# Hybrid decoder trunk on one Trainium2 core: the last norm's weights go into the gate matrix, and the low halves move to GpSimd

## The reference, cut to what matters

```python
def rms_norm(x, g):
    xf = x.astype(jnp.float32)
    y = xf * lax.rsqrt(jnp.mean(xf * xf, axis=-1, keepdims=True) + EPS)
    return (y * g.astype(jnp.float32)).astype(x.dtype)
...
        h = h + moe_out.reshape(bsz, s, d)
        u = rms_norm(h, norm_ple_g[l])
        ple_gate = jax.nn.sigmoid((u @ w_ple_gate[l]).astype(jnp.float32)).astype(h.dtype)
        h = h + ple_gate * (p[l] @ w_ple[l])
    return rms_norm(h, final_norm_g)
```

## Time and profile before

| what | value |
|---|---|
| three timed runs | 902.76, 903.9, 904.63 us (median 903.9) |
| profiled execution, its own time | 903.69 us |
| its span in the profile | 901.9 us |
| PE busy | 845.4 us, 94% of the span |
| DVE, ACT, POOL busy | 338.2, 262.3, 86.7 us |
| HBM | 247.41 MB read, 286 GB/s over the span |
| tail, from the first restore (827.1) to the end of the last product (894.5) | 67.4 us |

### The profile page before, as it was taken

How to read it: one execution, slowest core, us unless ns; L and a number is a source line. 1 busy time by engine, 2 the same in 40 slices (tenths; PEclk the granted TensorE clock), 3 DMA queues, 4 the chain that set the end, 5 groups by cost and what they waited for, 6 DMA issues and landing times.

```text
span 901.9 us, 10174 instructions
## 1 busy us (share of the span) xinstructions
PE 845.4 (94%) x4223; PEld 526.7 (58%) x4223; DVE 338.2 (37%) x462; ACT 262.3 (29%) x372; POOL 86.7 (10%) x63
## 2 busy tenths in 40 slices
PE   4999899999999999899999999888998897998896
PEld 3778687778888888635535344352352343533585
DVE  6699518952762526511110110101100101014975
ACT  7565326633432326302010100101001001013646
POOL 3429470000000000000000000000000000000000
PEclk9999999999999999999999999999999998999999
DMA  9222222211523772999999999999999999998802
GB/s 259 88 94 93 94 94 94 93 47 47 187 93 134 298 301 79 377 430 427 409 423 430 428 427 427 426 429 428 426 427 428 428 427 428 429 420 316 303 0 94
DMA packets 44758, 254.37 MB, mean 282 GB/s; under 512 B 8676, under 2 KB 9768, under 8 KB 31912
## 3 DMA queue, kind: packets, MB, share of 16 engines
q1 hardware_dynamic: 42120, 248.47, 68.2%
q0 software_dynamic: 2304, 4.20, 1.2%
q10 hardware_dynamic: 288, 1.05, 0.3%
HBM read 247.41 MB, written 10.49 MB: 286 GB/s over the span
## 4 chain that ended last, share of the span: by engine, by line
PE 68%; DMA 17%; DVE 10%; ACT 2%; issue 2%; SPq 1%; DVEq 0%; ACTq 0%
PE bank L1301 66%; DMA ring<-in_w_down_e_dram 11%; DMA ring<-in_w_up_e_dram 3%; DMA ring<-in_p_dram 2%; DVE ring L1007 1%; DVE ring L1011 1%; DVE r L1234 1%; SPq L461 1%; PE bank L1500 1%; DVE r L1013 1%; DMA r<-in_x_dram 1%; PE bank L1314 1%; DVE ring_rounded L382 0%; DVE r L1239 0%; DVE r L945 0%
## 5 line engine op out<-in xcount | busy, mean ns | idle before, releaser
L1301 PE MATMUL bank<-ring_rounded,ring_rounded 128*128 128x512 f32 x736 | 250.8, 395 | 3.7 <-DVE ring_rounded L953 3.7
L1301 PE MATMUL bank<-r_rounded,ring_rounded 128*128 128x512 f32 x736 | 243.8, 399 | 4.8 <-DVE ring_rounded L382 2.8
L1301 PEld LDWEIGHTS bank<-r_rounded,ring_rounded 128*128 128x128 f32 x736 | 139.5, 190 | 38.0 <-DVE ring_rounded L382 3.6
L1301 PEld LDWEIGHTS bank<-ring_rounded,ring_rounded 128*128 128x128 f32 x736 | 139.8, 190 | 35.3 <-issue 6.3
L1301 PE MATMUL bank<-ring,gain 128*64 128x512 f32 x472 | 118.0, 603 | 8.5 <-issue 4.9
L1301 PE MATMUL bank<-ring,hT 128*64 128x512 f32 x400 | 113.8, 628 | 6.4 <-DMA ring<-in_w_down_e_dram 6.4
L1301 PE MATMUL bank<-ring,junk 128*64 128x512 f32 x472 | 115.4, 592 | 0.0
L655 POOL DMA_INDIRECT expert_rows<-r,row_i x16 | 15.6, 977 | 674.1 <-DVE r L1200 398.3
L1301 PEld LDWEIGHTS bank<-ring,gain 128*64 128x64 f32 x472 | 35.5, 138 | 75.9 <-issue 67.7
L1301 PEld LDWEIGHTS bank<-ring,junk 128*64 128x64 f32 x472 | 37.0, 137 | 72.1 <-issue 72.0
L1301 PEld LDWEIGHTS bank<-pick,r_rounded 128*128 128x128 f32 x576 | 72.6, 199 | 9.9 <-issue 8.5
(11 more groups left out here) (204 smaller groups left out, 729.8 us busy)
## 6 DMA issues: line engine op xcount, KB each, us to landing
ring<-in_w_up_e_dram SPq DMA_DIRECT2D x31, 2048.0 KB, 29.0
ring<-in_w_gate_e_dram SPq DMA_DIRECT2D x25, 2048.0 KB, 27.4
ring<-in_w_down_e_dram SPq DMA_DIRECT2D x22, 2048.0 KB, 31.9
ring<-in_w_in_dram SPq DMA_DIRECT2D x18, 1024.0 KB, 7.3
r<-in_w_down_e_dram SPq DMA_DIRECT2D x5, 2048.0 KB, 33.0
r<-in_w_gate_e_dram SPq DMA_DIRECT2D x5, 2048.0 KB, 28.1
ring<-in_w_down_e_dram SPq DMA_DIRECT2D x7, 1024.0 KB, 21.9
r<-in_x_dram SPq DMA_DIRECT2D x8, 512.0 KB, 8.0
```

The source lines that it names most:

```text
L1301: return nc.tensor.matmul(*a, **k)
```

## The change

It does six things, all in the tail.

1. The stream itself is transposed, without the norm. Its root factor becomes the `scale` operand of the sigmoid, one per token, and DVE takes one reciprocal for all four tiles instead of four. The four passes of `normalise` over 128x1024 go.
2. The norm's weights are multiplied into the gate matrix: quarters 0 and 1 by ACT (four `Copy` with a scale per partition each, ahead of `gate_high`), quarters 2 and 3 by POOL (one multiply of 128x2048 each). For that the rows of the matrix are laid out as `(p k)` instead of `(k p)`, and the transposes read the stream with the same stride. The weights now come as 128x8 (`gain_col`) instead of 128x1024.
3. The low parts of quarters 0 and 1 are taken by POOL instead of DVE. Those of quarters 2 and 3 stay with DVE.
4. SP loads `p` ahead of `w_ple`, and quarter 1 right behind quarter 0, ahead of the scatter's end. PE waits for `p` and for `w_ple` separately.
5. The products of `p` use four banks instead of six, and the first stream transposes stand between product 5 and product 6.
6. In the last loop the squares of the first halves come one product later, and one `tensor_scalar` serves all four tiles. The results are written where the first expert outputs lay.

The diff, cut to its core:

```diff
         def ple_bank(q):
-            return bank[q % 6]
+            return bank[q % 4]
...
-            wg = w_ple_gate[0].rearrange("(k p) n -> p k n", p=P)
+            wg = w_ple_gate[0].rearrange("(p k) n -> p k n", p=P)
...
-                    sp.dma_start(wple, w_ple[0].rearrange("(k p) n -> p k n", p=P)).then_inc(ple_in, 16)
-                    sp.dma_start(p_rows, p[0, 0].rearrange("(i p) n -> p i n", p=P)).then_inc(ple_in, 16)
+                    sp.dma_start(p_rows, p[0, 0].rearrange("(i p) n -> p i n", p=P)).then_inc(p_in, 16)
+                    sp.dma_start(wple, w_ple[0].rearrange("(k p) n -> p k n", p=P)).then_inc(wple_in, 16)
                     wait_expert_read(max(range(8, 3 * NE, LEAD)))
                     load_gate(0)
+                    load_gate(1)
...
-                if i == 1:
-                    load_gate(1)
...
# POOL, behind the expert loop
+            for step in range(2):
+                gate_low(pool, nc.gpsimd, step, first_low_ready)
+            for step in range(2, 4):
+                h, ks = gate_steps[step]
+                pool.wait_ge(pg_in[step], 16)
+                nc.gpsimd.tensor_tensor(gate_part("whole", h)[:, ks, :], gate_part("whole", h)[:, ks, :],
+                                        gain_col[:, ks].unsqueeze(2).to_broadcast([P, KD // 2, HALF]),
+                                        ALU.mult).then_inc(pg_scaled, 1)
...
# ACT
             def gate_high(step):
                 h, ks = gate_steps[step]
-                act.wait_ge(pg_in[step], 16)
+                if step < 2:
+                    act.wait_ge(gain_in, 32)
+                    act.wait_ge(pg_in[step], 16)
+                    for k in range(ks.start, ks.stop):
+                        whole_k = gate_part("whole", h)[:, k, :]
+                        ins = nc.scalar.activation(whole_k, whole_k, ACT.Copy, scale=gain_col[:, k:k + 1])
+                    after(ins)
+                else:
+                    act.wait_ge(pg_scaled, step - 1)
...
-            for q in range(4):
+            for q in range(3):
                 copy_ple(q)
-            norm_h2(0)
+            gate_high(1)
+            copy_ple(3)
+            copy_h2T(0)
             copy_ple(4)
             copy_ple(5)
-            norm_h2(1)
+            norm_h2(0)
             copy_ple(6)
             copy_ple(7)
-            gate_high(1)
-            copy_u3T(0)
+            norm_h2(1)
+            copy_h2T(1)
+            norm_h2(2)
+            norm_h2(3)
             gate_high(2)
-            copy_u3T(1)
-            norm_h2(2)
+            copy_h2T(2)
+            gate_sigmoid(0)
             gate_high(3)
-            copy_u3T(2)
-            norm_h2(3)
-            copy_u3T(3)
+            copy_h2T(3)
...
# DVE
             add_y(0)
             add_y(1)
-            dve.wait_ge(gain_in, 32)
-            normalise_u3(0)
-            gate_low(dve, v, 0)
-            normalise_u3(1)
-            split_u3(0)
-            gate_low(dve, v, 1)
+            split_h2(0)
             add_y(2)
-            split_u3(1)
-            normalise_u3(2)
             add_y(3)
-            split_u3(2)
-            normalise_u3(3)
-            gate_low(dve, v, 2)
-            split_u3(3)
-            gate_low(dve, v, 3)
-            dve.wait_ge(h2_ready, TT)
+            split_h2(1)
+            dve.wait_ge(std_done, 2 * TT)
+            v.reciprocal(rstd[:, 2 * TT:3 * TT], std[:, 2 * TT:3 * TT]).then_inc(h2_rstd_ready, 1)
+            gate_low(dve, v, 2, second_low_ready)
+            split_h2(2)
+            gate_low(dve, v, 3, second_low_ready)
+            split_h2(3)
...
# PE
+            for q in range(6):
+                ple_product(q)
+            transpose_h2(0)
+            ple_product(6)
+            ple_product(7)
             for q in range(2 * TT):
                 ple_gate(q)
```

More of the change, by code:

```diff
@@ L575, in _ @@
                 sp.wait_ge(final_ready, q + 1)
-                sp.dma_start(out[0, i * P:(i + 1) * P, part], u3[:, i, part]).then_inc(stored, 16)
+                sp.dma_start(out[0, i * P:(i + 1) * P, part], result(i)[:, part]).then_inc(stored, 16)
             sp.wait_ge(stored, 16 * 2 * TT)
@@ L888, in norm_h2, with copy_h2T, gate_sigmoid @@
                 norm(2 * TT + i, h1[:, i, :])
[L890 to L894 removed]
+            def copy_h2T(i):
+                copy_transposed(2 * (TT + i), h2T_high, (4, 5, 6, 7))
+                copy_transposed(2 * (TT + i) + 1, h2T_high, (4, 5, 6, 7))
+            def gate_sigmoid(q):
+                act.wait_ge(pg_psum, q + 1)
+                if q == 0:
+                    act.wait_ge(h2_rstd_ready, 1)
+                if q >= 2:
+                    act.wait_ge(h3_ready, q - 1)
+                n = 2 * TT + q % TT
+                nc.scalar.activation(psig[:, q % 2, :], bank[q % 4][:, :], ACT.Sigmoid, scale=rstd[:, n:n + 1]).then_inc(pg_sig, 1)
@@ new lines, in _ @@
+            copy_h2T(3)
+            for q in range(1, TT):
+                gate_sigmoid(q)
+                first_square(q - 1)
+            first_square(TT - 1)
+            for q in range(TT, 2 * TT):
+                i, n = q % TT, 2 * TT + q
+                gate_sigmoid(q)
+                after(nc.scalar.activation(std[:, n:n + 1], eps[:, :], ACT.Sqrt))
+                act.wait_ge(h3_ready, q + 1)
+                after(nc.scalar.activation(junk[:, HALF:D], h1[:, i, HALF:D], ACT.Square, accum_out=ssq[:, i:i + 1]))
+                act.wait_ge(half_bias, 1)
+                nc.scalar.activation(std[:, n:n + 1], ssq[:, i:i + 1], ACT.Sqrt, bias=rstd[:, i:i + 1],
+                                     scale=1.0 / D).then_inc(std_done, 1)
@@ L1584, in _, with transpose_h2, ple_product, ple_gate @@
             ins.then_inc(pT_psum, 1)
-            def transpose_u3(i):
-                transpose_rows(2 * (TT + i), u3, (4, 5, 6, 7))
-                transpose_rows(2 * (TT + i) + 1, u3, (4, 5, 6, 7))
+            def transpose_h2(i):
+                pe.wait_ge(h2_ready, i + 1)
+                for h in range(2):
+                    q = 2 * i + h
+                    if q >= 4:
+                        pe.wait_ge(ut_low, 2 * TT + q - 3)
+                    for k in range(4):
+                        ins = nc.tensor.transpose(bank[4 + q % 4][:, k * P:(k + 1) * P], h1_by_k(i)[:, 4 * h + k, :], ident[:, :])
+                    ins.then_inc(ut_psum, 1)
+            def ple_product(q):
+                i, h = q // 2, q % 2
+                if q >= 4:
+                    pe.wait_ge(ple_ready, q - 3)
+                for k in range(KP):
+                    ins = mm(ple_bank(q)[:, :], pT[:, k, i * P:(i + 1) * P], wple[:, k, h * HALF:(h + 1) * HALF],
+                             start=(k == 0), stop=(k == KP - 1))
+                ins.then_inc(ple_psum, 1)
+            def ple_gate(q):
+                h, i = q // TT, q % TT
+                pe.wait_ge(ut_low, 2 * (TT + i + 1))
+                if q < TT:
+                    pe.wait_ge(ple_ready, TT + q + 1)
+                else:
+                    pe.wait_ge(pg_sig, q - 3)
+                cols = slice(i * P, (i + 1) * P)
+                for k in range(KD):
+                    if k == KD // 2 and q < TT - 1:
+                        transpose_h2(q + 1)
+                    if i == 0 and k % (KD // 2) == 0:
+                        pe.wait_ge((first_low_ready, second_low_ready)[h], k // (KD // 2) + 1)
+                    wh, wl = gate_part("high", h)[:, k, :], gate_part("low", h)[:, k, :]
+                    for p_, (still, stream) in enumerate(((h2T_high, wh), (h2T_high, wl), (h2T_low, wh))):
+                        ins = mm(bank[q % 4][:, :], still[:, k, cols], stream, start=(k == 0 and p_ == 0),
+                                 stop=(k == KD - 1 and p_ == 2))
+                ins.then_inc(pg_psum, 1)
             pe.wait_ge(y_stored, rounds * NE + 2)
@@ L1593, in _ @@
             pe.wait_ge(pT1_ready, 1)
[L1594 to L1624, removed]
+            pe.wait_ge(wple_in, 16)
+            for q in range(6):
[3 more added lines that the diff above has]
+            ple_product(7)
             for q in range(2 * TT):
-                if q == 0:
-                    pe.wait_ge(ple_ready, 2 * TT)
                 ple_gate(q)
```

63 lines of the change are left out of this document (26 added, 37 removed).

## The result

The changed kernel takes 910.66 us (median of five runs, 910.46 to 913.5) against 903.9 before: the ratio is 1.0083, with a 95% interval of 1.0064 to 1.0103. It is slower, by 6.8 us. The profiled execution took 910.92 us with a span of 908.8, against 903.69 and 901.9.

What follows compares the result with a forecast made beforehand. DVE was taken to set when the gate products start, PE the end from there. The profiled 903.69 us plus 8.3 for the later second product and 0.1 for the scaled sigmoid gave 912.1 us, range 906 to 916.5.

Steps and rivals of the forecast that it cites:

- DVE sets the start of the products, PE the end: In the tail, DVE decides when gate products start; from 846.5 us on PE is full and sets the end.
- POOL and DVE exclude each other, and all four passes hit: Tail: each POOL pass shuts out a DVE operation with two SBUF inputs; four passes cost 17.0 us; chance 0.68.
- the sum: DVE's path to the second gate product: 826.5 + 8.2 + 9.84 + 17.04 + 1.29 = 862.9 us.
- The case at 55.80: Mixing stage before the change: DVE's L1011 takes 4.95 us beside a POOL pass, 0.69 without; read as exclusion.
- The operation at 19.32: Before the change: a DVE operation on eight columns takes 1.57 us, ending with POOL's pass; read as exclusion.
- 4.26 us a pass: Cost to DVE of each POOL pass in the tail, taken as 4.95 - 0.69; four passes cost 17.0 us.
- Restores from 826.5: DVE's restores start at 826.5 us instead of 827.1, waiting for POOL to release the row buffer behind its last scatter.
- The second product at 862.9: Second gate product on PE starts at 862.9 us against 854.6 before, 8.3 us later.
- the dearest rival: Exclusion costs 5.16 us a pass and one more low-clock stretch adds 1.7: 917.4 us; chance 0.10.
- DVE keeps its place while it has work: Rival: POOL gets in only where DVE waits; third product starts 5.4 us later, 909.2 us; chance 0.12.
- No exclusion: Rival: POOL's tail passes don't block DVE; third product starts 3.2 us earlier, 900.6 us; chance 0.10.
- Behind the second product: Third product at 869.2 us finds its quarter 2 ready at 868.5; quarter 3 and the rest hide behind products.

Runs made afterwards that it cites:

- d_reads: The kernel before plus eight POOL multiplies of 128x1024 behind the last scatter, results unused: 916.81 us, ratio 1.0149.
- e_writes: The kernel before plus 18 POOL memsets of 128x1024 behind the last scatter, results unused: 902.93 us, ratio 0.9998.
- h_lows_only: The kernel before with only the low parts of quarters 0 and 1 moved from DVE to POOL: 908.71 us, ratio 1.0047.
- g_reordered: The changed kernel without POOL passes in the tail, ACT's quarter 2 work ahead of two norms, further ACT and DVE reordering: 900.69 us, ratio 0.9975.
- b_scale_act: The changed kernel with quarters 2 and 3 scaled by ACT instead of POOL: 910.34 us, ratio 1.0072 to the kernel before.
- f_loads: The kernel before with only the load order changed (p ahead of w_ple, quarter 1 right behind quarter 0): 905.18 us, ratio 1.0011.

## Why the prediction was right, point by point

- **DVE sets the start of the products, PE the end.** Right. Everything behind the start of the second product cost the same as before but for its first twelve matmuls and 0.1 us of the sigmoid.
- **POOL and DVE exclude each other, and all four passes hit.** Right, and shown apart from all else by d_reads and e_writes. Four long operations were forecast, and there are four. But they are not the ones that I had named. The two low parts were to hit the third and fourth restore; the restores were done by then, and all four passes hit adds. Besides the earlier restores (below), the first low part began a little late, at 833.09 and not at 832.3, since ACT's scaled copies waited for `gain_col` up to 828.51. That changed nothing in the sum, since all of these stand ahead of tile 1's low part. It did change PE's idle time: the first stream transposes waited 2.77 us and not some 8, as only one pass stood ahead of tile 0's adds.
- **What the rows of before showed.** The case at 55.80 is the pattern that came. The operation at 19.32 is not: L968 multiplies one SBUF tile by a constant. It has one SBUF input, and it waited for POOL's pass all the same. So "both inputs in SBUF" was too narrow a reading of these rows; for the tail nothing hung on it, as restores and adds have two.
- **4.26 us a pass.** Too high as a mean. By the chain the four long adds cost 3.8, 4.3, 2.2 and 3.2 us over their 1.22: 13.5 instead of 17.0. The first pass fell partly on a wait of DVE's for expert rows (0.57 us), the third ran beside L990 for 1.28. And the scale pass, for which I had only the low part's row, is shorter: 3.72 us for the first, against 4.53 for a low part. Whether the multiply or its broadcast operand makes it shorter isn't shown; the multiplies of d_reads, without a broadcast operand, were short as well. The full price appears where DVE had work ready all through: 4.3 here, 4.05 in h_lows_only.
- **Restores from 826.5.** They started at 824.94; 0.5 of that is the mark, which came earlier in this execution. I had the release of the row buffer behind the 0.96 us of the last scatter's issue; but by the records POOL's queue gave it at about 824.7, before that instruction began to run at 824.86. What came late next was another wait: the first expert rows, 0.57 us at 833.1.
- **The second product at 862.9.** It started at 859.4: 1.6 for the restores and 3.5 for the passes too many, less 0.6 for the wait for expert rows, and less 1.2 for a term that the sum left out. The low part of tile 0 (L990, 1.28 us at 846.61) stands in DVE's stream between the adds of tile 1 and those of tile 2, and the sum has the low part of tile 1 alone. The first product was done by then, as forecast, but by 3.2 us and not by 0.8.
- **The clock.** I left the low clock out of the sum and gave it to the dearest rival, at 1.7 us. It came: PE had been idle for 3.2 us, the granted clock was 1.00 up to 859.4 and 0.55 on average from 859.42 to 861.7, and the first half of the second product took 4.62 instead of 2.73 (+1.9). Some 0.3 of this is not the clock: in g_reordered the same twelve took 3.03 at a granted clock of 1.00. So against 8.4 us of the sum stand 5.3 + 1.9 + 0.1; errors of opposite sign made the total look better than its terms, and that part is luck.
- **The rivals.** That DVE keeps its place while it has work is refuted: the pass at 838.92 waited for one add only, though the next was ready. No exclusion is refuted by the whole of the above. The dearer rival had half of what happened: the low clock came, the dearer passes did not.
- **Behind the second product** nothing waited for ACT, as forecast. But in b_scale_act I then read ACT's order wrongly and missed by 4 us.

## What to carry to other kernels

Before work is moved from a busy VectorE to an idle GpSimd, look for both in the same stretch of a trace: if VectorE's operations with two SBUF inputs stretch there, the move costs VectorE the whole pass (4.05 to 4.3 us for a low part of 128x2048, where VectorE has such work ready), more than the 2.3 us that the same pass takes on VectorE itself. A busy share doesn't show it; the duration of a single instruction does. In these runs memsets on GpSimd, VectorE operations with an input in PSUM, and ScalarE's scaled copies were free of it. The copies of quarter 1 ran in the middle of POOL's first low part and took the 2.56 us that they take alone:

```profile
834.35 2.56 ACT L895 ACTIVATE ring<-ring,gain_col 128x512 f32<-128x512 f32 x4
```

An input less is no safe sign, though: L968 waited with one SBUF input. And when a sum follows one engine's stream, count every instruction that stands in it: the prediction missed one.

## What the runs showed that I had not expected

- 18 memsets on POOL beside the same adds cost nothing (ratio 0.9998).
- A POOL multiply of 128x2048 with one broadcast operand is shorter than the low part's subtraction: 3.72 us against 4.53, and two in 8.27 us beside DVE's adds.
- In d_reads a POOL multiply of 128x1024 cost DVE 1.5 us, less than half of what a low part of 128x2048 costs.
- In the changed kernel's trace POOL's queue is ahead of its engine: a release that stands behind a scatter's issue was given at 824.7, before that issue ran at 824.86.
- A load put beside a scatter stretches it: 6.19 us from issue to landing in f_loads, where 4.5 us after that issue SP could go on before. In the five other kernels that load quarter 1 early it took 5.0 to 6.1; in the four that don't, 4.4 to 4.8.
